# Stream offset 192, two weight sums moved to GpSimd in layer 0, and block closings of one step per unit

## The reference, cut to what matters

```python
# first block, layer i (two layers); mod = silu(c) @ ada_w[i] + ada_b[i]
x = x + gt1 * y                                  # y: a conv mixer, then an RWKV mixer
h = _modulate(_rmsnorm(x, norm_g[i, 1]), sh2, sc2)
x = x + gt2 * (jnp.square(jax.nn.relu(h @ mlp_w1[i])) @ mlp_w2[i])
# second block: two of these
x = x + 0.5 * ((jax.nn.silu(h @ w_gate) * (h @ w_up)) @ w_down)
# and cross attention: kv = m @ wkv, with m = rmsnorm(mem, mem_norm), 256 tokens
```

## Time and profile before

| | us |
|---|---|
| median of 3 runs (lowest, highest) | 2511.47 (2507.17, 2514.07) |
| the profiled execution, its own time | 2506.6 |
| its span, first to last instruction | 2504.8 |
| PE busy | 2442.9 (98%) |
| DVE busy | 1628.0 (65%) |
| ACT busy | 1072.9 (43%) |
| POOL busy | 222.5 (9%) |
| mean granted TensorE clock | 0.992 of full speed (2.4 GHz) |

### The profile page before, as it was taken

One profiled execution on the slowest core, in us unless ns is written; L12 is line 12 of the kernel. 1 busy time (PEld: TensorE's weight loads), 2 busy tenths in 40 slices (PEclk: granted clock), 3 DMA queues, 4 the chain that ended last, 5 costly groups with the idle time before them and its releaser, 6 DMA issues.

```text
span 2504.8 us, 44071 instructions
## 1 busy us (share of the span) xinstructions
PE 2442.9 (98%) x18636; PEld 2084.5 (83%) x18636; DVE 1628.0 (65%) x2639; ACT 1072.9 (43%) x1686; POOL 222.5 (9%) x226
## 2 busy tenths in 40 slices
PE   8999999999999999999999999999999999999998
PEld 7887989876777887798989889889668987889888
DVE  7867978667845445676759657566345744557557
ACT  4225453327643233554456333344256444334334
POOL 0100000100220000000000010111321000011010
PEclk9999999999999999999999999999999999999999
DMA  8664555661210003255545336345212431336335
GB/s 313 197 191 140 168 189 187 195 206 68 93 35 4 4 6 134 77 159 138 130 132 137 105 114 170 96 124 162 67 51 68 137 108 47 97 109 161 117 94 139
DMA packets 101060, 304.67 MB, mean 122 GB/s; under 512 B 11280, under 2 KB 13584, under 8 KB 100352
## 3 DMA queue, kind: packets, MB, share of 16 engines
q1 hardware_dynamic: 80944, 237.38, 29.2%
q0 software_dynamic: 19920, 64.48, 10.7%
HBM read 297.62 MB, written 4.19 MB: 120 GB/s over the span
## 4 chain that ended last, share of the span: by engine, by line
PE 86%; DVE 8%; ACT 3%; issue 2%; DMA 1%; SPq 0%; DVEq 0%; ACTq 0%
PE ps L782 19%; PE ps L788 16%; PE ps L786 16%; PE ps L833 5%; PE ps L838 5%; PE ps L836 5%; PE ps L801 3%; PE ps L798 3%; DVE WLs L2079 2%; PE ps L845 1%; ACT WHs L1405 1%; PE ps L987 1%; PE ps L1000 1%; DVE ada L2117 1%; PE ps L952 1%
## 5 line engine op out<-in xcount | busy, mean ns | idle before, releaser
L2079 DVE TENSOR_TENSOR WLs<-raw,WHs 128x1024 fp32r<-128x1024 f32 (+3 forms) x498 | 510.8, 1026 | 271.4 <-ACT WHs L1405 267.3
L782 PE MATMUL ps<-HH,WHs 128*128 128x512 f32 x1728 | 655.1, 400 | 6.2 <-ACT HH L1485 3.7
L1405 ACT ACTIVATE WHs<-raw 128x1024 fp32r<-128x1024 f32 (+3 forms) x516 | 455.1, 883 | 331.7 <-PE ps L838 145.2
L788 PE MATMUL ps<-HH,WLs 128*128 128x512 f32 x1462 | 570.4, 390 | 2.8 <-DVE WLs L2079 2.8
L786 PE MATMUL ps<-HL,WHs 128*128 128x512 f32 x1462 | 569.4, 389 | 0.0
L782 PEld LDWEIGHTS ps<-HH,WHs 128*128 128x128 f32 x1728 | 324.2, 188 | 78.6 <-issue 13.6
L833 PE MATMUL ps<-HT,WHs 128*128 128x256 f32 x1344 | 377.5, 281 | 4.1 <-DVE X L2166 4.0
L838 PE MATMUL ps<-HT,WLs 128*128 128x256 f32 x1344 | 375.5, 279 | 3.2 <-DVE WLs L2079 2.9
L836 PE MATMUL ps<-HT,WHs 128*128 128x256 f32 x1344 | 374.7, 279 | 0.0
L788 PEld LDWEIGHTS ps<-HH,WLs 128*128 128x128 f32 x1462 | 274.4, 188 | 62.3 <-DVE WLs L2079 4.6
L786 PEld LDWEIGHTS ps<-HL,WHs 128*128 128x128 f32 x1462 | 274.8, 188 | 56.1 <-issue 2.2
(11 more groups left out here) (463 smaller groups left out, 3669.0 us busy)
## 6 DMA issues: line engine op xcount, KB each, us to landing
ada<-in_adaw POOLq DMA_DIRECT2D x80, 512.0 KB, 4.7
raw<-in_f1gu_b SPq DMA_DIRECT2D x20, 512.0 KB, 3.6
raw<-in_f2gu_b SPq DMA_DIRECT2D x20, 512.0 KB, 3.5
raw<-in_f1gu_a_m SPq DMA_DIRECT2D x18, 512.0 KB, 3.5
raw<-in_w_in_m SPq DMA_DIRECT2D x18, 512.0 KB, 3.5
raw<-in_f2gu_a_m SPq DMA_DIRECT2D x18, 512.0 KB, 3.5
ada<-in_adaw SPq DMA_DIRECT2D x16, 512.0 KB, 16.7
raw<-in_cw_in_m SPq DMA_DIRECT2D x16, 512.0 KB, 3.7
```

The costliest lines, as they stand in the source:

```text
L782: pe.matmul(o[m], WHs[:, s, w], hi, start=k == 0, stop=False)
L788: t = pe.matmul(o[m], WLs[:, s, w], hi, start=False, stop=k == DEPTH_K[name] - 1)
L1405: act.activation(WHs[:, SLOT[v], 0:n], piece(v), ACT.Copy).then_inc(*S.up("w_hi", ("hi", v)))
L2079: dve.tensor_tensor(WLs[:, s, 0:n], piece(v), WHs[:, s, 0:n].bitcast(F32), SUB).then_inc(*S.up("w_lo", ("lo", v)))
```

## The change: what it does

1. HT and HT0 start at WK+32960 (= 32768+192) in place of +64. wsum0 and the ada tiles move up by 128 bytes to make room. MNs moves from WK+81920 to WK+32960.
2. In layer 0 POOL makes S1 and S3 of each pair (`summed`), between its ada loads: those of pair a of mw2_0a before the load of tile 52+a, those of mw2_0b before tile 66+a. VectorE no longer makes them. q0 is now counted as read when the low split of unit 1 is done, in all quads.
3. The ada dots beside mw2_0a and mw2_0b stand at i = 3, 10, 17, 24 and 26.
4. Closings are queued step by step: one step per unit, on ScalarE and on VectorE, from unit 1 of the next pair on; what is left is done after the last unit.

```diff
-        return ("lo", unit_of(v, [0, 1, 4, 5, 6][q]))
+        return ("lo", unit_of(v, [1, 1, 4, 5, 6][q]))
...
-        HT = at_("HT", WK + 32832, [128, 2, 6, 1792], F32R)
+        HT = at_("HT", WK + 32960, [128, 2, 6, 1792], F32R)
...
-        HT0 = at_("HT0", WK + 32832, [128, 2, 5, 1792], F32R)
-        wsum0 = at_("wsum0", WK + 104512, [128, 640])
+        HT0 = at_("HT0", WK + 32960, [128, 2, 5, 1792], F32R)
+        wsum0 = at_("wsum0", WK + 104640, [128, 640])
...
-        ada = at_("ada", WK + 107072, [128, NADA, 1024])
+        ada = at_("ada", WK + 107200, [128, NADA, 1024])
...
-        MNs = at_("MNs", WK + 81920, [128, 2, 8, 256], F32R)
+        MNs = at_("MNs", WK + 32960, [128, 2, 8, 256], F32R)
...
                 def evac(m):
...
                     a, i = m
                     if m == (0, 3):
                         warm(ACT.Sqrt)
                     last = m == (BLOCKS[name] // 2 - 1, 6)
+                    if i and waiting:
+                        waiting.pop(0)()
+                    for n, b in closed(m):
+                        waiting.extend(close(n, b))
+                    while last and waiting:
+                        waiting.pop(0)()
...
-                    if v + 1 < len(WANT) and WANT[v + 1][1] == "s" and WANT[v + 1][3] in (SUMMED if v < HALT else (2, 6)):
+                    if v + 1 < len(WANT) and WANT[v + 1][1] == "s" and WANT[v + 1][3] in (2, 6):
                         sum_quarters(v + 1)
...
-                if i == 1:
-                    on.wait_ge(*S.at("raw", v0, 0))
-                    on.wait_ge(*S.at("raw", v0, 1))
-                    dve.tensor_tensor(quarter(v0, 1), quarter(v0, 1), quarter(v0, 0), ADD).then_inc(*S.up("w_sum", ("sum", v)))
-                if i == 4:
-                    on.wait_ge(*S.at("raw", v0, 2))
-                    on.wait_ge(*S.at("raw", v0, 3))
-                    dve.tensor_tensor(quarter(v0, 2), quarter(v0, 2), quarter(v0, 3), ADD).then_inc(*S.up("w_sum", ("sum", v)))
...
-                        draw(name, *m)
-                        for n, b in waiting:
-                            close(name, n, b)
-                        waiting[:] = closed(m)
-                        if m == (BLOCKS[name] // 2 - 1, 6):
-                            for n, b in waiting:
-                                close(name, n, b)
+                        a, i = m
+                        draw(name, a, i)
+                        if i and waiting:
+                            waiting.pop(0)()
+                        for n, b in closed(m):
+                            waiting.extend(close(name, n, b))
+                        while waiting and m == (BLOCKS[name] // 2 - 1, 6):
+                            waiting.pop(0)()
...
-                        dense(two, last_lows(one)(residual(two)), (lambda i: after(i) if i in (10, 12, 17, 19, 24) else None) if after else None)
+                        dense(two, last_lows(one)(residual(two)), (lambda i: after(i) if i in (3, 10, 17, 24, 26) else None) if after else None)
...
+            def summed(name, a):
+                v = UNIT[name, a, 0]
+                on.wait_ge(*S.at("raw", v, 0))
+                on.wait_ge(*S.at("raw", v, 1))
+                pool.tensor_tensor(quarter(v, 1), quarter(v, 1), quarter(v, 0), ADD).then_inc(*S.up("g_sum", ("sum", v + 1)))
+                on.wait_ge(*S.at("raw", v, 2))
+                on.wait_ge(*S.at("raw", v, 3))
+                pool.tensor_tensor(quarter(v, 2), quarter(v, 2), quarter(v, 3), ADD).then_inc(*S.up("g_sum", ("sum", v + 4)))
...
+            sums = {52: ("mw2_0a", 0), 53: ("mw2_0a", 1), 54: ("mw2_0a", 2), 55: ("mw2_0a", 3),
+                    66: ("mw2_0b", 0), 67: ("mw2_0b", 1), 68: ("mw2_0b", 2), 69: ("mw2_0b", 3)}
             for u in range(16, 96):
+                if u in sums:
+                    summed(*sums[u])
                 on.wait_ge(*(S.at("dot", u - NADA) if u >= 16 + NADA else S.at("ada", 7)))
```

More of the change, by code:

```diff
@@ L516, in build @@
         names += ["w_lo", "w_sum", "w_added1_0", "w_added1_1", "w_added2_0", "w_added2_1", "v_const", "v_mod", "v_norm", "v_in", "v_evac", "v_mix", "v_scan", "v_attn"]
-        names += ["g_mix", "g_scan", "g_ffn", "g_lo"]
+        names += ["g_mix", "g_scan", "g_ffn", "g_lo", "g_sum"]
         S = Signals({n: ctx.enter_context(nc.semaphore("s_" + n)) for n in names})
@@ L1454, in residual, with close, first @@
                 waiting = []
-                def evac(m):
+                def close(n, m):
                     _, to, tag = RESIDUAL[name]
[L1458 to L1464, removed]
-                        if m == (BLOCKS[name] // 2 - 1, 6):
[L1466 to L1469, removed]
+                    def first():
@@ L1470, in evac, with second @@
                         on.wait_ge(*S.at("X", to, m))
                         square(tag, n, X[:, m])
[L1472 to L1478, removed]
+                    def second():
+                        act.activation(HH[:, m], X[:, m], ACT.Identity,
+                                       scale=gains(name)[:, m:m + 1]).then_inc(*S.up("a_in", ("HH", tag, m)))
@@ new lines, in third, with evac @@
+                    def third():
+                        if n:
+                            on.wait_ge(*S.at("acc2", n - 1))
+                        act.activation(r1, X[:, m], ACT.Square, scale=vc("final_g", m)).then_inc(*S.up("a_norm", ("sq2", n)))
+                    return [first] + [second] * (name in GAINS) + [third] * (name == "mw2_1c")
+                def evac(m):
+                    if not RESIDUAL[name][2]:
+                        return
+                    if not isinstance(m, tuple):
+                        if m == 0:
+                            warm(ACT.Sqrt)
+                        for step in close(m, m):
+                            step()
+                        return
+                    a, i = m
+                    if m == (0, 3):
+                        warm(ACT.Sqrt)
+                    last = m == (BLOCKS[name] // 2 - 1, 6)
+                    if i and waiting:
[4 more added lines that the diff above has]
+                        waiting.pop(0)()
@@ L2191, in evac @@
                                              op1=ADD).then_inc(*S.up("v_evac", ("X", to, m), ("free", name, m)))
-                    close(name, m, m)
+                    for step in close(name, m, m):
+                        step()
                 return evac
@@ L2197, in close, with first, second @@
                 tag = RESIDUAL[name][2]
-                if tag:
+                def first():
                     add_square(tag, n)
-                if name in GAINS:
+                def second():
                     on.wait_ge(*S.at("HH", tag, m))
@@ L2203, in close, with third @@
                                              op0=MUL, op1=SUB).then_inc(*S.up("v_in", ("HL", tag, m)))
-                if name == "mw2_1c":
+                def third():
                     on.wait_ge(*S.at("sq2", n))
@@ L2210, in close @@
                         dve.tensor_tensor(acc2, acc2, r1, ADD).then_inc(*S.up("v_norm", ("acc2", n)))
+                return ([first] if tag else []) + [second] * (name in GAINS) + [third] * (name == "mw2_1c")
             def scaled(tag, f, dst, scalar):
```

## The result

The changed kernel takes 2528.53 us (2528.05 to 2529.41, 4 runs) against 2512.77 us before (2507.17 to 2517.27, 4 runs): the ratio is 1.0076, with a 95% interval from 1.0059 to 1.0094. It is slower by about 19 us by the ratio (0.0076 × 2513), where 2495.5 was forecast, and outside the range of 2485 to 2514.

A forecast was written before the change was run, and what follows sets the result against it. TensorE, busy 98%, was taken as the bound. From 2506.6 us profiled, -11.8 (HT offset), -2.5 (MNs), -1.2 (sums on GpSimd) and -0.5 (closings) gave 2490.6; the same 16.0 from 2511.5 gave 2495.5, range 2485 to 2514.

The forecast's parts named there:

- S1 and S3 on GpSimd: Layer 0's quads: two sums per pair moved off VectorE, with one dot per pair, -1.2 us (from -3.5 to +7.6).
- one split and one sum held: Layer 0: of 3.1 us of GpSimd sums per pair, VectorE loses 1.4 us.
- my 12.0: VectorE's need per pair of layer 0 after the change, 12.0 us, against 12.35 or 11.9 for the pair.
- rival 4: Layer 0: GpSimd holds VectorE for all 3.1 us of each pair, +7.6 us; 2504 with good offset, 2519 without; chance 0.12.
- one dot per pair: Layer 0: each pair has one ada dot on VectorE, which with two sums fewer needs about 10.6 us before holds.
- First pairs: Layer 0's first pairs: S1 late and S3 holding VectorE delay draw 2, +2.7 us for both parts; pairs near 15 us.
- The offset: HT and MNs matmuls: starts at the fast pace, 0.1135 us, in place of 0.1176 and 0.1200; -11.8 and -2.5 us.
- rival 2: HT and MNs streams: a mixture of phases gives half of the gain, -9 us, 2502; chance 0.10.
- The next place in that direction: HT streams: going from 0 to 64 helped, so 192, again not on a multiple of 128, should give 0.1135 us.
- The four later pairs: Layer 0's four pairs of 13.2 to 13.4 us lose what they have above 12.35, -3.9 us.
- The closings: Pairs of mw2_1c: spreading the steps saves only the burst, -0.5 us (0 to -1); the step behind the last unit costs 0.
- The six later loads and the ada tiles: Loads behind a part's last pair, one unit later through q0's release, and ada loads queued behind sums: 0.

## Why the prediction was wrong

**The step that failed** is the term "S1 and S3 on GpSimd", -1.2 us, which was +26 us on the quads of layer 0 and +29 us with its own kernel. Three things in it:

- *"I count one split and one sum held, 1.4 us."* I let VectorE's split, which starts ahead of GpSimd's add, finish. The rows say that it is held until both adds are done: 4.20 us, 3.4 of them lost (the earlier trace rows showed a split that began near an add's end, and so only the last 0.3 us of this). Beside one add it takes 2.71 us, beside one-column adds 0.82.
- *What is queued behind.* I wrote that draws are not held, since they read PSUM. No run tried that for a draw itself, but VectorE works in order, and draw 4 stands behind the held split. The need per pair (my 12.0, or 13.75 in rival 4) is a sum; the time came from one position, where TensorE's unit 6 waits for draw 4. With 3.4 us lost before that draw the wait is 3.12, so the slack there was some 0.3.
- *The clock.* Each of the six waits, of 2.9 to 3.9 us, was followed by 3.4 us at half clock, 1.6 us more each time: about 10 us. No term of mine had it, though rival 4 had long waits.

Rival 4 named this mechanism and priced it at +7.6 us, from the need of the whole queue and without the clock; its size was a third of what came, and its chance, 0.12, was too low. My "one dot per pair" holds for three of the four pairs only, and the low end of the range adds up to 2489.5 from my own terms, not to 2488; neither changes the outcome.

**First pairs.** The cause was as forecast (S1 late, S3's hold at once on S2), the size was not: 20.0 and 18.5 us against my 15. ScalarE's wait for S1 was 3.1 us, S2 took 2.18 us, and then the pair had the same long split (4.18 us) and a wait of 3.9 us before unit 6.

**The offset.** Forecast -14.3 us; measured -11 by the ratio (-7 to -16). So the gain is real and near, but the reason was half right, and that the forecast came near is in part luck. I took 0.1135 throughout; rival 2 had a mixture of phases and half the gain, 7 us for the offset, at a chance of 0.10, and the paces in the traces (5.6 us in the quads, 1.0 in wkv) fit that better. In fact 64 and 192 share both phases, 0.1133 and 0.1177, and 192 falls into the fast one more often: 1422 to 2200 of 4032 in eight executions, against 66 to 523 in four at 64. Pairs that begin without a stall, as in f1d_a and f2d_a, stayed slow in all. At 0 and 128 there is no fast phase: 0.1200 at 0, 0.118 to 0.121 at 128. "The next place in that direction" was no argument: 64 and 192 share their phases and differ in the odds, and no run says why. Nor does the pace change only behind a stall, as I had read it from the trace before. In the changed kernel's last pair of mw2_0a, where TensorE waits for nobody, 29 steps of 0.1134 are followed by 13 of 0.1177:

```profile
323.73 0.28 PE L833 MATMUL ps<-HT,WHs 128*128 128x256 f32 x1
...
327.02 0.28 PE L838 MATMUL ps<-HT,WLs 128*128 128x256 f32 x1
...
327.26 0.28 PE L836 MATMUL ps<-HT,WHs 128*128 128x256 f32 x1
...
328.79 0.28 PE L838 MATMUL ps<-HT,WLs 128*128 128x256 f32 x1
```

The Trainium skill, "TensorE: Matmul & The Clock Gate" (Step-by-step), names independent read ports for the two operands. What I drew from it, that the place would not matter, is not so here: the same matmul has three paces, and the offset alone moves the kernel by 0.46%. Whether the ports have to do with it no run shows.

**The four later pairs.** Their stalls did go (in the last pair of mw2_0a, 13.2 us, TensorE waits for nobody; the half clock at its start is what is slow), but the dots' places do that alone: 12.3, 12.4 and 12.4 us with all four sums on VectorE.

**The closings.** Forecast -0.5, measured 0.0 (-0.1% to +0.1%). I gave the extra step behind the last unit nothing; it took back some 0.8 of the 1.6 us that the spreading had saved in the trace, and a half-clock stretch that is not its doing hid the rest there. The six later loads and the ada tiles cost nothing that a row shows, as forecast.

Part by part the ratios give -0.46% (offset), +1.14% (sums with dots) and 0.01% (closings), +0.7% in all, against +0.76% measured.

## What to carry to other kernels

Before work goes from VectorE to GpSimd, look at what VectorE runs at that moment: float32 work with two SBUF inputs on VectorE did not run beside GpSimd's adds here, and the held instruction delayed all that stood behind it. Price the delay at the one instruction that TensorE waits for, not by the engine's load, and look whether a half clock can follow: here it added nothing to the six waits of 1.6 to 2.5 us with one add, and 1.6 us to each of the six of 2.9 to 3.9 with two. If the added operand comes from HBM anyway, an adding DMA did the sum here for the price of its issue. Whether the adds would have been free at another place in VectorE's queue was not tried. And try the cheap part first: moving the dots alone took the stalls away that the sums were to remove.

## What the runs showed of the hardware

- A VectorE split of 640 columns with two SBUF inputs took 0.82 us alone, 1.10 beside 128-column GpSimd adds (but the sum S2, held through five of them, 2.73), 2.71 beside one add of 1.57 us and 4.20 beside two in a row; by the records it was held although it began 0.46 us before the add. GpSimd's starts in the records are rough, so that order is sure only as far as they are. The Trainium skill, "SBUF — State Buffer" (SBUF: two separate sides), calls the port pair that the two engines share an exclusive lock: whichever of them starts first has it for the whole instruction, and the other is blocked. The trace agrees that with whole adds one of them stops rather than slows (GpSimd's took 1.57 us beside the split as without it). As the records stand it differs on who: by that rule a split that starts first, at 291.80, would have been done in 0.82 us.
- DMA issues of GpSimd, 0.53 us and more each, did not lengthen a split: in the two executions with adding DMAs 67 splits of 640 columns had only such issues beside them, and took 0.83 us at most.
- 256-column matmuls of full clock came mostly at 0.1133, 0.1177 or 0.1200 us, by the place of the moving tensor. At one place two paces alternated, behind stalls but also without one (at 327 us above), and in two executions of one program the shares of the paces differed.
- In the quads of layer 0 a half clock of 3.4 us followed each TensorE wait of 2.9 to 3.9 us before unit 6 in the changed kernel (six of six), and none of the six of 1.6 to 2.5 us with S3 alone on GpSimd. At 1366 us it also came, in the kernel with the offset alone, where TensorE waited for nobody.
